# Prompt attention of a hybrid decoder layer: a couple's output product is issued behind the next step's small turn instead of ahead of it

## The reference

```python
def block(args):
    i, ql_b, qp_b = args                       # 128 query positions
    mask = key_pos[None, :] <= q_pos[:, None]
    s = (jnp.einsum('bqhl,bkl->bhqk', ql_b, c_kv)
         + jnp.einsum('bqhr,bkr->bhqk', qp_b, k_pe)).astype(jnp.float32) * MLA_SCALE
    s = jnp.where(mask, s, -jnp.inf)
    prob = jax.nn.softmax(s, axis=-1).astype(c_kv.dtype)
    return jnp.einsum('bhqk,bkl->bqhl', prob, c_kv)
...
o_mla = jnp.einsum('bthl,lhv->bthv', ctx_lat, W['mla_w_uv']).reshape(B, T, MLA_HEADS * V_HEAD) @ W['mla_w_o']
```

## Time and profile before

| What | Value |
|---|---|
| Median of 3 runs | 3077.56 us (3075.92 to 3082.49) |
| The profiled execution's own time | 3077.9 us |
| Its span in the profile | 3076.2 us |
| PE busy in the span | 2942.2 us, 96% |
| DVE, ACT, POOL busy | 59%, 37%, 26% |
| Steps 0 to 31 of the prompt's attention in the span | about 1455 us to 1632 us |
| PE and ACT busy from 1455 us to 1640 us | 167.39 us and 113.07 us of 185 us |
| Mean granted TensorE clock of the whole execution | 0.981 |

### The profile page before, as it was taken

One profiled execution on the slowest core, in us unless ns is written; L12 is line 12 of the kernel. 1 busy time (PEld: TensorE's weight loads), 2 busy tenths in 40 slices (PEclk: granted clock), 3 DMA queues, 4 the chain that ended last, 5 costly groups with the idle time before them and its releaser, 6 DMA issues. The chain is left out here.

```text
span 3076.2 us, 65641 instructions
## 1 busy us (share of the span) xinstructions
PE 2942.2 (96%) x27498; PEld 2783.6 (90%) x27498; DVE 1807.0 (59%) x2868; ACT 1133.8 (37%) x2186; POOL 796.7 (26%) x884
## 2 busy tenths in 40 slices
PE   8999999999999989979999989999998999999998
PEld 8999999999999988838777579999998999999998
DVE  7877774575636556676554552343324877776555
ACT  5433334443113233345664351221144433334443
POOL 3555451033001133240003000000015455553103
PEclk9999999999999999989999999999998999999999
DMA  6566668563422120011106641212123456666763
GB/s 173 175 196 204 190 196 253 178 205 110 147 65 70 54 80 4 18 43 33 34 24 196 212 168 42 52 42 66 32 79 101 127 184 196 200 198 213 237 204 113
DMA packets 416767, 393.37 MB, mean 128 GB/s; under 512 B 50616, under 2 KB 367841, under 8 KB 415706
## 3 DMA queue, kind: packets, MB, share of 16 engines
q1 hardware_dynamic: 383450, 277.05, 30.1%
q0 software_dynamic: 31984, 112.13, 11.0%
q10 hardware_dynamic: 1040, 0.00, 0.0%
HBM read 283.59 MB, written 105.53 MB: 126 GB/s over the span
## 5 line engine op out<-in xcount | busy, mean ns | idle before, releaser
L2159 PE MATMUL banks<-hid_pieces,dn_high 128*128 128x258 f32 x2464 | 444.6, 283 | 0.2 <-DVE dn_part L2135 0.2
L1907 PE MATMUL banks<-x_pieces,gate_pieces 128*128 128x258 f32 x3360 | 415.3, 283 | 2.1 <-DVE sq L2001 1.3
L1907 PE MATMUL banks<-x_pieces,up_pieces 128*128 128x258 f32 x3360 | 414.4, 283 | 0.2 <-DVE sq L2001 0.2
L1907 PEld LDWEIGHTS banks<-x_pieces,gate_pieces 128*128 128x128 f32 x3360 | 408.8, 189 | 2.9 <-DVE sq L2001 1.9
L1907 PEld LDWEIGHTS banks<-x_pieces,up_pieces 128*128 128x128 f32 x3360 | 408.6, 189 | 0.4 <-DVE sq L2001 0.4
L2159 PEld LDWEIGHTS banks<-hid_pieces,dn_high 128*128 128x128 f32 x2464 | 378.8, 188 | 0.4 <-DVE dn_part L2135 0.4
L2159 PE MATMUL banks<-hid_pieces,dn_part 128*128 128x258 f32 x1232 | 345.8, 281 | 0.0
L1167 PE MATMUL banks<-XG,pR 128*128 128x344 f32 (+1 forms) x1800 | 288.1, 320 | 2.5 <-DVE pR L2701 1.4
L1167 PEld LDWEIGHTS banks<-XG,pR 128*128 128x128 f32 (+1 forms) x1800 | 281.8, 187 | 9.4 <-issue 6.1
L1167 PE MATMUL banks<-XR,mg_gate 128*128 128x344 f32 x1728 | 284.9, 321 | 1.3 <-PEq L53 1.3
L1167 PEld LDWEIGHTS banks<-XR,mg_gate 128*128 128x128 f32 x1728 | 275.4, 189 | 1.6 <-issue 1.6
(11 more groups left out here) (569 smaller groups left out, 5513.7 us busy)
## 6 DMA issues: line engine op xcount, KB each, us to landing
hid_spill<-h_stage SPq DMA_DIRECT2D x44, 516.0 KB, 3.8
dn_low<-w_sums SPq DMA_DIRECT2D x32, 384.0 KB, 3.6
praw<-in_w_in SPq DMA_DIRECT2D x24, 512.0 KB, 4.2
sq<-in_w_in SPq DMA_DIRECT2D x24, 512.0 KB, 4.0
late<-hid_spill POOLq DMA_DIRECT2D x42, 258.0 KB, 3.6
t_sums<-late POOLq DMA_DIRECT2D x42, 258.0 KB, 2.9
sq<-in_ffn_down POOLq DMA_DIRECT2D x42, 256.0 KB, 3.8
w_sums<-sq POOLq DMA_DIRECT2D x42, 256.0 KB, 2.9
```

The source lines that it names most:

```text
L1907: ins = k.nc.tensor.matmul(out, self.w[m][:, a, w, f * P:(f + 1) * P], self.x[p][:, b, x, f * TQ:(f + 1) * TQ], start=first and f == 0 and ...
L2159: ins = k.nc.tensor.matmul(k.ps[2 * j + q][:, 0:TQ], a[s][:, f * P:(f + 1) * P], k.hid_pieces[m % 2][:, q, f, b, :], start=m in self.FRESH ...
```

## The change

Fourteen of the sixteen outputs are issued one PE step later: `output(n // 2 - 1)` stands behind `turn(n, 2)` of the next, even step n, and ahead of `score(n + 2, 1)`. The outputs behind step 15 (ahead of the values) and behind step 31 (the last) stay where they were. Only PE's order changes, with its list of steps; the orders of ACT, DVE, SP and POOL, all waits and all sizes stay.

```diff
     for n in range(LAST):
         more = n + 2 < LAST
-        pe_steps += [("t", n, 2)] + ([("s", n + 2, 1)] if more else []) + [("t", n, 0), ("t", n, 1)]
+        pe_steps += [("t", n, 2)]
+        pe_steps += [("o", n // 2 - 1)] if n % 2 == 0 and n and n != LAST // 2 else []
+        pe_steps += ([("s", n + 2, 1)] if more else []) + [("t", n, 0), ("t", n, 1)]
...
-        pe_steps += [("o", n // 2)] if n % 2 else []
+        pe_steps += [("o", n // 2)] if n in (LAST // 2 - 1, LAST - 1) else []
...
             for n in range(LAST):
                 turn(n, 2)
+                if n % 2 == 0 and n and n != LAST // 2:
+                    output(n // 2 - 1)
                 if n + 2 < LAST:
                     score(n + 2, 1)
...
-                if n % 2:
+                if n in (LAST // 2 - 1, LAST - 1):
                     output(n // 2)
```

## The result

The changed kernel took 3085.29 us (median of 11 runs, 3080.81 to 3089.82), the kernel before, measured beside it, 3079.12 us (11 runs, 3074.68 to 3083.32). The ratio is 1.002 with a 95% interval of 1.0012 to 1.0028: slower by about 6.2 us, 3.7 to 8.6. The forecast was 3.2 us slower, and a time of 3080.8 in a range up to 3084.2. The sign was right, the size was not: the time lies above the range, and the interval leaves out both the 3.2 us and the "no change that it can tell". A part of the miss is not the change's: the forecast was built on 3077.56 for the kernel before, which took 1.6 us more in this series.

A forecast was written before the change was run, and what follows sets the result against it. The prediction took a loop through ACT, DVE and PE's output as the bound; turns ahead of outputs added 1.20 + 1.64 + 0.16 + 0.20 = 3.2 us to 3077.56, giving 3080.8, in a range from 3076.5 to 3084.2.

The forecast's parts named there:

- no change that it can tell: Whole kernel: 3.2 us slower (0.10%) lies under the 0.2%, 6.2 us, that a measurement can tell; chance 0.85.
- The loop: Each couple is paced by ACT to DVE to ACT to PE's output to ACT, 9.45 us from copy to copy.
- The turn can't fill the wait: PE before the output: the small turn waits for the same copy that releases the output, so idle time stays.
- The PE time of the turns: Small turns ahead of outputs: about 0.10 us a block, 3.2 us in all where the loop is closed.
- The switch of the array: PE from transposition to the output's 64-column weights: bounded between nothing and 0.25 us each, taken as nothing.
- The cover in the couples with keys: Outputs 2, 6 and 10: a 0.20 us delay is hidden by ACT's 0.23 wait for DVE; otherwise 0.60 us.
- The second: Rival: 14 switches between last transposition and output drain PE, 0.25 us each, 6.6 us slower, 3084.2; chance 0.12.
- The first: Rival: PE is the bound and the turn fills its wait before outputs, at most 3.2 us faster, 3074.4; chance 0.07.
- the fourth: Rival: the change does nothing, through slack on ACT or DVE or a shorter later PE wait, 3077.6; chance 0.13.
- The third: Rival: PE's clock falls once more, over the keys and output 2, costing 2.4 us, 3083.2; chance 0.05.

The follow-up runs named there:

- experiment 3: ACT computes the large tile's next exponential ahead of its output wait in 11 couples: on the kernel before, ratio 0.9988; on the changed kernel, 1.000.
- experiment 1: Kernel before plus idle PE products behind the last output, in groups and in turn: 0.26 us a switch with transpositions, 0.28 with 512-column products.
- experiment 4: Changed kernel, ACT copying the small turn ahead of its output wait, with a second buffer: ratio 1.0009; with the early exponential too, 0.9988.
- both moves: Changed kernel with ACT's small-turn copy and, in 11 couples, the large tile's next exponential ahead of its output wait: ratio 0.9988 to the kernel before.

## Why the prediction was right or wrong

- **The loop.** Right in what it said of the change: PE's idle time stayed where it was, moved to the turn, and what stands between the release and the output is paid by the couple. Too simple in one thing: the loop is not alone. PE's own path was only 0.29 shorter in the couple of experiment 3, and a step that ACT takes ahead of its wait can make the output's copy late. For a change that lengthens the loop this made no difference.
- **The turn can't fill the wait.** Right: 0.25, 0.78 and 0.61 before the small turns, against 0.77 before output 1 and the like.
- **The PE time of the turns.** Right: 0.10 a block.
- **The switch of the array.** This is the step that failed: "I take nothing, since output 2 is the switch in question, in the same direction, with no wait between." It costs 0.15 into the output behind a transposition, 11 x 0.15 = 1.65, and the way from the output's start to the next score is 0.02 to 0.03 longer than it was to the next turn (2.52 against 2.50 for output 1; 3.39 against 3.36 for output 0, which started at 1465.13 before). 3.2 + 1.65 + 11 x 0.02 = 5.1, against 5.0 measured in the loop. The row was misread: that output 2 started before the modelled end of the keys shows nothing, because that end is modelled. The other row, the turn that started before the modelled end of output 1, shows as little: that is the way back, 0.38 in experiment 1. Starts would have shown it. The timeline of PE in the kernel before, output 0 and then the end of the keys, read in windows so narrow that single products are listed:

```profile
1465.13 3.43 PE L4472 MATMUL banks<-mla_pT,mla_v 128*64 128x256 f32 x20 [0.24 <-ACT mla_pT L4501]
...
1486.70 0.63 PE L4379 MATMUL banks<-XR,mla_w 128*128 128x512 f32 x2
...
1486.93 0.40 PE L4379 MATMUL banks<-XR,mla_w 128*128 128x512 f32 x1
1487.25 0.43 PE L4472 MATMUL banks<-mla_pT,mla_v 128*64 128x256 f32 x1
```

  The last two keys started 0.23 apart (1486.70 and 1486.93), and output 2 started at 1487.25, 0.32 behind the last of them, 0.09 more. So part of the price already stood in the trace of the kernel before, in the very stretch of the earlier trace rows. The Trainium skill (TensorEngine Tiling (Array Packing), Key Properties) has the rule that a change of tiling mode drains the engine; by that rule a switch behind other work costs, and the trace agrees, at 0.15 here and at 0.26 to 0.28 for the mean of both directions in experiment 1. That what PE does there is a drain is not shown. The rule stood in the prediction, and was set aside on a row that couldn't carry it.
- **The cover in the couples with keys.** Right in the number, with luck in the size: copies 2, 6 and 10 come 0.22 later, and 0.22 comes back at the next copy. The 0.20 was the turn without a switch. What was added is 0.31 from the turn's start to the output's, less the 0.08 that the output behind the keys had paid before. With 0.15 for the switch and nothing off, the cover of 0.23 would not have held.
- **Rivals.** The second (the switch drains PE) was right that the switch costs PE time ahead of the output, and high in its price, 0.25 against 0.15. The first and the fourth fell: the loop became longer in every kind of couple that was closed. The third did not occur in the changed kernel, whose clock fell at the last output alone, as before. In experiment 4 the clock fell where PE's idle time had been joined into one piece, in both runs. But in three runs of experiments 3 and 4 (all but the one with both moves) it also fell ahead of copy 0, behind instructions that the kernel before has too. So a fall needs no change of PE's order, and what decides it stays open.
- **What stays open.** The loop accounts for 5.0 us and the runs say 6.2, with 3.7 to 8.6, which takes in the 5.0. Whether the rest belongs to the change is not shown: the profile has 4.8 us more ahead of the loop and 2.6 less behind it, in code that did not change.

## What to carry to other kernels

Before work is moved into a wait, look at what releases the wait and what releases the work: where it is the same event, the work is not hidden but put in front of what the others wait for. Cost a change of product shape on PE from starts, never from modelled ends, and in the place where it will stand: here it was 0.15 behind transpositions and 0.08 to 0.09 behind the keys. And a step that is finished earlier on one engine gains nothing until the engine that consumes it is told to take it earlier.

## What the runs showed that was not expected

- A switch between products with 128 and with 64 columns of weights costs 0.26 to 0.28 us on average over both directions, 0.15 to 0.19 into the 64 columns and 0.38 back, and a product of 512 columns ahead of it does not hide it.
- The 14 distances repeated to 0.02 us in the one run that has the same instructions there, while whole runs of the kernel before spread over 9 us (3074.68 to 3083.32); where the clock holds, one profile's distances were a sharper measure of this change than 11 runs. A sum that leaves out the first and the last couple can leave out a fall of the clock, though.
- The last output took 4.84 us at a clock that had fallen. In experiment 1's run the clock did not fall there, and the distance from copy 14 to copy 15 was 8.22 instead of 9.64, with the same instructions up to that point: 1.4 us from the clock alone. The same instructions ran at either clock ahead of copy 0 as well (15.52 us from the table's load before, 16.84 in experiment 3).
